# Zero matmuls that open the PSUM accumulations of the input projection and of the RWKV-7 state, in a hybrid encoder layer

## What is computed

```python
xn = rmsnorm(x, norm_mix)                       # x: (1, 256, 2048)
pA, pB, pC, pD = split(xn @ w_in)               # w_in: (2048, 6400)
y = concat([rwkv7_mixer(pA), chunk_band_attention(pB), diff_attention(pC), short_conv_mixer(pD)])
x = x + y @ w_out                               # w_out: (2048, 2048)
x = x + hier_moe(rmsnorm(x, norm_ffn))          # 32 experts, hidden 256, top 2 of the best group of 8
return rmsnorm(x, norm_final)

def rwkv7_step(state, inp):                     # one frame; 8 heads of 64
    r, w, k, v, a, b = inp
    sa = einsum('bhvk,bhk->bhv', state, a)
    state = state * w[:, :, None, :] + sa[..., None] * b[:, :, None, :] + v[..., None] * k[:, :, None, :]
    return state, einsum('bhvk,bhk->bhv', state, r)
```

## The kernel before

| place | granules |
|---|---|
| start, around the small matmuls of the low-rank gates (L941 to L960) | 0 to 32 |
| bonus and transposes (L968, L977, listed as L859) | 33 to 35, behind one transpose pair each |
| Gram matrices (L999, L1007) | 36 to 39 |
| inversion, `t1(i)` (L1022) then `xu(i - 1)` (L1038, L1039), ten rounds | 40 + i; then 50 |
| first matmuls of the state stage (L1057) | 51 behind them |
| four chunks c of the recurrence (L1072 to L1099), three granules each | 52 to 63; then 64, 65 |
| eight band-attention heads, two granules each | 66 to 81 |
| four differential-attention heads, three granules each, and after them | 82 to 93; 94 to 96 |
| no work between them | 97 to 99 |

## Time and profile before

### The profile page before, as it was taken

One profiled execution on the slowest core, in us unless ns is written; L12 is line 12 of the kernel. 1 busy time (PEld: TensorE's weight loads), 2 busy tenths in 40 slices (PEclk: granted clock), 3 DMA queues, 4 the chain that ended last, 5 costly groups with the idle time before them and its releaser, 6 DMA issues.

```text
span 1020.4 us, 18209 instructions
## 1 busy us (share of the span) xinstructions
PE 970.7 (95%) x8066; PEld 749.1 (73%) x8066; DVE 446.6 (44%) x699; ACT 274.2 (27%) x445; POOL 73.3 (7%) x81
## 2 busy tenths in 40 slices
PE   4999897999989998999999999999999999999995
PEld 4999897989989998978888656656565656566542
DVE  4758956444565556665434114141313223141404
ACT  4555342222325455544531001010101000010103
POOL 5010002213010000430000000000000000000000
PEclk9999999999999998999999999999999999999998
DMA  9675442223233443589969899999999999999992
GB/s 270 192 248 162 149 140 83 85 85 125 89 119 125 124 141 108 181 266 355 365 228 358 340 419 430 427 426 426 428 425 429 426 426 428 427 426 427 425 381 87
DMA packets 83458, 285.80 MB, mean 280 GB/s; under 512 B 5756, under 2 KB 57032, under 8 KB 70960
## 3 DMA queue, kind: packets, MB, share of 16 engines
q1 hardware_dynamic: 79344, 279.98, 71.2%
q0 software_dynamic: 1824, 4.04, 1.6%
q10 hardware_dynamic: 2208, 0.57, 0.3%
HBM read 280.36 MB, written 4.22 MB: 279 GB/s over the span
## 4 chain that ended last, share of the span: by engine, by line
PE 84%; DVE 8%; ACT 2%; POOL 2%; issue 2%; DMA 1%; DVEq 0%; ACTq 0%; POOLq 0%
PE bank L1293 22%; PE bank L906 20%; PE bank L1314 10%; PE bank L1266 6%; PE bank L923 3%; PE bank L925 3%; PE bank L924 3%; PE bank L859 2%; PE bank L1275 2%; DVE ring_r L1483 2%; PE bank L1327 1%; PE bank L1276 1%; PE bank L1022 1%; PE bank L868 1%; PE bank L1193 1%
## 5 line engine op out<-in xcount | busy, mean ns | idle before, releaser
L906 PE MATMUL bank<-xTr,hi 128*128 128x256 f32 x1344 | 255.1, 291 | 5.1 <-DVE ring_r L1483 5.1
L1293 PE MATMUL bank<-arena 128*64 128x256 f32 x2048 | 232.0, 381 | 1.0 <-DVE arena L1886 1.0
L1483 DVE TENSOR_TENSOR ring_r<-arena,hi 128x1024 fp32r<-128x1024 f32 x132 | 162.5, 1241 | 148.5 <-ACT hi L593 146.7
L906 PEld LDWEIGHTS bank<-xTr,hi 128*128 128x128 f32 x1344 | 214.4, 196 | 11.3 <-DVE ring_r L1483 5.7
L1293 PEld LDWEIGHTS bank<-arena 128*64 128x64 f32 x2048 | 144.6, 137 | 81.5 <-issue 14.2
L906 PE MATMUL bank<-xTr,ring_r 128*128 128x256 f32 x672 | 192.7, 287 | 0.0
L593 ACT ACTIVATE hi<-arena 128x1024 fp32r<-128x1024 f32 x132 | 138.5, 1060 | 109.7 <-PE bank L906 79.9
L906 PEld LDWEIGHTS bank<-xTr,ring_r 128*128 128x128 f32 x672 | 131.9, 196 | 0.0
L1314 PE MATMUL bank<-arena,const 128*64 128x512 f32 x448 | 100.8, 597 | 0.0
L1882 DVE TENSOR_TENSOR arena<-arena,bank 128x512 f32<-128x512 f32 x60 | 63.9, 1111 | 40.6 <-PE bank L1276 40.6
L1314 PEld LDWEIGHTS bank<-arena,const 128*64 128x64 f32 x448 | 30.3, 137 | 54.5 <-issue 52.0
(11 more groups left out here) (310 smaller groups left out, 943.1 us busy)
## 6 DMA issues: line engine op xcount, KB each, us to landing
arena<-in_expert_w_gate SPq DMA_DIRECT2D x32, 2048.0 KB, 21.4
arena<-in_expert_w_up SPq DMA_DIRECT2D x32, 2048.0 KB, 20.6
arena<-in_expert_w_down SPq DMA_DIRECT2D x26, 2048.0 KB, 21.6
arena<-in_w_in SPq DMA_DIRECT2D x50, 1024.0 KB, 5.3
arena<-in_w_out SPq DMA_DIRECT2D x16, 1024.0 KB, 7.2
arena<-in_expert_w_down SPq DMA_DIRECT2D x12, 1024.0 KB, 20.0
arena<-in_x SPq DMA_DIRECT2D x2, 1024.0 KB, 8.5
arena<-in_x SPq DMA_DIRECT2D x4, 512.0 KB, 8.8
```

Of the source, the lines that this page charges most:

```text
L906: ins = MM(PJ[n % 2][:, h * U:(h + 1) * U], a, b, start=h + q + tt + k == 0, stop=h == 1 and q == 3 and tt == 3 and k == 2)
L1293: ins = MM(bank[2 + st_][CAP * a:CAP * a + CAP, c // 2 * U:(c // 2 + 1) * U], xg[:, t, CAP * a:CAP * a + CAP], slot(b + a)[:, t * U:(t + 1 ...
L1483: TT(ring_r[:, n % 2, q, :], ring[:, n % 2, q, :], hi[:, g % NHI, :].bitcast(f32), ALU.subtract).then_inc(s["lo_done"], 1)
```

## The change

Each accumulation is now opened by a matmul of zero weights with `start=True` that writes the whole bank (or half bank), and all matmuls that carry data have `start=False`. In the input projection `clear` is issued at quarter 0 of each of the 25 units: 128x128 zero weights as float32r, 512 moving columns. In the state stage `clear_half` (float32, 64 zero columns of weights, all 128 rows) is issued 8 times with 512 moving columns ahead of L1057, and twice with 256 ahead of the products of each of the chunks 0 to 2. The output is the same.

```diff
+            def clear(b_):
+                MM(b_[:, :], zeros[:, :], xTr[:, 0, 0:2, :], start=True, stop=False)
+            def clear_half(b_, n):
+                MM(b_, zeros[:, 0:CH].bitcast(f32), nat[:, 2, 0, 0:n], start=True, stop=False)
...
             def in_granule(n, q):
...
+                if q == 0:
+                    clear(PJ[n % 2])
...
-                            ins = MM(PJ[n % 2][:, h * U:(h + 1) * U], a, b, start=h + q + tt + k == 0,
+                            ins = MM(PJ[n % 2][:, h * U:(h + 1) * U], a, b, start=False,
...
             pe.wait_ge(s["xu_ev"], 17)
+            for b_ in K[0:4]:
+                for a in range(2):
+                    clear_half(b_[chunk(a), :], 512)
...
                             ins = MM(K[2 * b + m][chunk(a), h * HD:(h + 1) * HD], NK[chunk(a), e, 2 * c + m, 1, b, :], v,
-                               start=h == 0, stop=b == 0 and m == 0 and a == 0 and h == 7)
+                               start=False, stop=b == 0 and m == 0 and a == 0 and h == 7)
...
                 if c < 3:
+                    for e in range(2):
+                        clear_half(K[5][chunk(e), 0:SEQ], SEQ)
...
-                        MM(K[5][keys_, t * HD:(t + 1) * HD], nat[rows, 1, m, h * HD:(h + 1) * HD], v, start=h < 2,
+                        MM(K[5][keys_, t * HD:(t + 1) * HD], nat[rows, 1, m, h * HD:(h + 1) * HD], v, start=False,
                            stop=False)
```

## The result

The changed kernel takes 1031.24 us (median of 4 runs, 1030.64 to 1032.56) against 1023.61 before (4 runs). The ratio is 1.008, 95% interval 1.0062 to 1.0097, so 8.2 us more, 6.3 to 9.9 (the medians differ by 7.6); the forecast was 9.1 more, 1032.6, in a range of 1029.0 to 1036.5. In a second set of runs, beside two of the experiments, it measured 1.0091 (1.0077 to 1.0105), which is 9.3 us more. The ratios leave out two disturbed executions, one of the kernel before with 1038.26 us and one of experiment 3 with 2473.78 us.

The account below looks back on a forecast made before the run. TensorE's instruction stream was taken to bound the kernel. Full clears 3.9, half-bank clears 3.6 and 1.35, and shape changes 0.3 made 9.1 us, added to the median 1023.5 for 1032.6 us; range 1029.0 to 1036.5.

Parts of the forecast that it names:

- The price of a full clear, 0.227 us: Input projection: each 512-column float32r clear costs 0.227 us, from output-projection matmul spacing; bounds 0.12 and 0.24 us.
- 17 on the path, 8 hidden: Input projection: 17 of 25 full clears delay the chain, 3.9 us together; 8 fall into TensorE's idle time.
- 3.6 us before the state products: Before L1057: eight 512-column half-bank clears at 0.447 us each, all on the path, 3.6 us.
- 1.35 for those in K[5]: Before L1078 in chunks 0 to 2: six 256-column half-bank clears at 0.225 us each, 1.35 us.
- 0.3 us for changes of shape: Before L1057 and in chunk 0: new matmul shapes cost between 0 and 2 x 0.20 us; 0.3 taken.
- Shifts on the way: Profile after: TensorE's work at 119.43 us comes 1.1 us later, L1057 at 234.93 about 5.7 us later.
- 441.58 moves by 9.1 us and the expert stage keeps its length: Output projection starts 9.1 us later; nothing behind 441.58 us absorbs lateness, and the expert stage's length is unchanged.
- a sign of being wrong: Output projection's start moving by less than its sum of clears, or the expert stage changing length, would refute the prediction.
- Rival 1: State stage: halves don't run side by side in clear_half; 6.3 us more than forecast, 1038.9 us; chance 7%.
- Rival 2: Cover lost, notably at 88 to 119 us: all 8 hidden clears count, 10.9 us more, 1034.4 us; chance 6%.
- Rival 3: Clears before 441 us are absorbed in unseen waits; time unchanged at 1023.5 us; chance 3%.
- Rival 4: Clears hold up the granted clock behind waits, recovering up to 4.6 us; 1024.1 or 1020.9 us; chance 2%.

Follow-up runs that it names:

- experiment 3: Kernel before plus four full clears in a row at each of the 8 units counted as hidden, none elsewhere: 1021.65 us, ratio 0.9993.
- experiment 1: Kernel before plus only the 25 full clears of the input projection, state stage as before: 1025.67 us, ratio 1.0042.
- experiment 4: Kernel before plus two full clears in a row at each of the 17 units counted as on the path, none elsewhere: 1031.41 us, ratio 1.0094.
- experiment 2: Kernel before plus only the 14 half-bank clears of the state stage, no full clears: 1027.45 us, ratio 1.0057.
- experiment 5: Kernel before plus only the half-bank clears, the first eight reordered, lower halves of four banks before upper halves: 1028.72 us, ratio 1.0069.
- experiment 6: Changed kernel with its fourteen half-bank clears replaced by seven whole-bank float32r clears: 1027.99 us, ratio 1.0056 to the kernel before.
- experiment 9: Zero matmuls before five TensorE waits, added to the changed kernel (1027.44 us, 1.0052) and to its variant with whole-bank float32r state-stage clears (1024.59 us, 1.0024).

## Why the prediction held, step by step

- **The price of a full clear, 0.227 us.** Right. Granule starts move by 0.22 to 0.25 us net at each that can be read; twice as many cost about twice as much (experiments 1 and 4). The rule cited from the Trainium skill, 131 ns for 512 columns in a stream (TensorE: Matmul & The Clock Gate, "Back-to-back issue gap"), would by my estimate have made the sum 17 x 0.131 + 5.25 = 7.5 us; the clears measured cost 0.22 to 0.25 us, and no row here shows such a spacing at 512 columns.
- **17 on the path, 8 hidden.** Right but for one. The 8 are hidden, shown by experiment 3. Granule 88 is hidden too: it stands in the chain at 400.63, but VectorE sets the time at 411.18 us. That leaves 16, and the sum is 0.2 us too high. Granule 40, which the chain lists and the idle time behind it contradicts, was among them: from granule 36 to 41 the run with four clears there fell back 0.58 us, the runs without any full clear 0.54 (experiment 2) and 0.83 (experiment 5).
- **3.6 us before the state products.** Measured 3.58 and 3.59. **1.35 for those in K[5]**: measured 1.42 with the change of shape in it.
- **0.3 us for changes of shape.** Too much: 0.57 - 0.43 = 0.14 in chunk 0, and nothing to see before L1057.
- **Shifts on the way.** 234.93 was to come 5.7 us later and came 5.46 and 5.38 later; 119.43 was to move by 1.1 us and moved by 0.15 and 0.03. Against experiment 3, which has no clear before either point but the hidden ones and the same head start, it is 5.9 and 5.8, and 1.1 and 1.0.
- **441.58 moves by 9.1 us and the expert stage keeps its length.** The second half is right (10.10 and 10.09); the stage has one more wait than the prediction names, 0.5 us for ScalarE at 990 us, the same in both kernels. The first half was not. The shift was 8.5 and 6.9 us in the two profiles, less than the sum of the clears, which is what the prediction had named as a sign of being wrong. It does not tell against the prices, since both are short because the profile before carries a half-clock stretch at 21 us that no other has (about 1 us), and because stretches at 120, 168, 304 and 397 us fall a little differently each time. The further 1.6 us came behind 441.58, in the output projection, where I had said that nothing would change. This is the step that was missing: the sum has no term for the clock behind the wait at 441.58. In the two profiles the missing 0.6 and 2.2 us before 441.58 and the 1.6 behind it are of opposite sign and end at 10.1 and 8.55. The parts alone, 16 x 0.23 + 3.59 + 1.42, give 8.7 us, between the 8.2 and 9.3 measured. So the prices are shown, and that the total came so near 9.1 is in part luck.
- **Rival 1** (halves not side by side): excluded for the order used. Its price was also mis-sized: a half clear that runs alone takes 0.86 us, not the 1.02 scaled up from L1088.
- **Rivals 2 and 3** (cover lost; absorbed): excluded by experiments 3 and 1. A little of rival 3 is true, at granule 88.
- **Rival 4** (the clears hold the clock up): the mechanism exists, and zero matmuls can do it; the clears themselves shortened the four waits by 0.1 to 0.3 us (the longest from 3.73 to 3.51) and left most of the stretches in place. 2.6 us were there to be had by it, not the 4.6 of my three rows, since the stretch at 397 us was worth nothing at the end.

What stays open: the profiles of the changed kernel (both), of experiment 1 and of experiment 4 have the half-clock stretch behind the wait at 441 us; those of the kernel before and of experiments 2, 3, 5 and 6 have not. TensorE waits there 1.83, 1.85, 1.83 and 2.09 us in the former, 2.09, 2.10, 1.16, 2.07 and 1.86 in the latter, so the length of the wait does not tell them apart. With the wait filled the stretch was not there (experiment 9); what decides without a filling was not found. Why the stretch at 168 us survived the filling before granule 39 stays open as well.

## What to carry over

Price an added matmul by the distance of starts of the nearest form, times those instances that are pieces of the chain and have no idle time of the engine directly behind them; the rest is free, and its cover can be tested by multiplying it. A piece in a half-clock stretch between two waits for another engine needs a second look: the slow stretch may only fill idle time, as at granule 88. If an accumulation has to be opened by a matmul of its own, take one over the whole bank in float32r. Idle time of TensorE can be worth filling with zero matmuls into an open accumulation, where its own work sets the time afterwards; read the granted clock by windows, before and behind each wait, to see where.

## What I had not expected of the hardware

- With all eight instructions of the lower halves ahead of the eight of the upper halves, four pairs still started 6 to 57 ns apart (experiment 5). By my reading, matmuls for the upper half started while earlier ones for the lower half had still to start.
- A wait of TensorE of about 2 us was followed by 3.4 us at half clock in four profiles and not in five others, with nearly the same work around it (2.09 us in one of either sort).
